# Routing of a one-core MoE layer: ties and counts by scans, slots summed once, the one-hot lanes in four strips, the first eight groups' row indices apart, and the register values of the expert loop by one load

## What is computed

```python
def hier_moe(x, p):                       # x: 640 tokens x 1024
    p_coarse = softmax(xt @ p['w_rc'] + p['b_rc'])            # 4 groups of experts
    p_grp, g_idx = lax.top_k(p_coarse, 1)                     # the first of equals wins
    l_fine = (xt @ p['w_rf'] + p['b_rf']).reshape(t, 4, 4)
    l_sel = take_along_axis(l_fine, g_idx[:, :, None], axis=1)[:, 0]
    top_l, e_idx = lax.top_k(l_sel, 2)                        # 2 experts of the group
    w_sel = softmax(top_l, axis=-1) * p_grp
    ...
    act = silu(xt @ w_gate[e]) * (xt @ w_up[e]) * gate        # 16 experts, 512 wide
    y = sum over e of act @ w_down[e]
```

## Time and profile before

| | us |
|---|---|
| median of 3 runs (1013.94 to 1014.93) | 1014.29 |
| the profiled execution | 1014.13 |
| its span, first to last instruction | 1012.0 |
| start of the routing on DVE (L1181), in the span | 660.94 |
| first matmul of the expert loop (L1743) | 693.42 |
| end of the last down matmul (L1754) | 965.86 |
| busy: PE / DVE / ACT / POOL | 867.5 / 410.3 / 264.3 / 103.9 |

### The profile page before, as it was taken

How to read it: one execution, slowest core, us unless ns; L and a number is a source line. 1 busy time by engine, 2 the same in 40 slices (tenths; PEclk the granted TensorE clock), 3 DMA queues, 4 the chain that set the end, 5 groups by cost and what they waited for, 6 DMA issues and landing times.

```text
span 1012.0 us, 17458 instructions
## 1 busy us (share of the span) xinstructions
PE 867.5 (86%) x6969; PEld 487.1 (48%) x6969; DVE 410.3 (41%) x792; ACT 264.3 (26%) x534; POOL 103.9 (10%) x199
## 2 busy tenths in 40 slices
PE   2998999999999999999874999635999999999910
PEld 0232455554454578444773445433555555555500
DVE  4445621222752922500564476261333333333345
ACT  0656311211110102121433132201333332333221
POOL 3100000000000000000101000002222222222140
PEclk9999999999999997989887999757999999999965
DMA  8964614043310020021203310595999999996162
GB/s 282 400 258 166 231 50 155 12 166 137 113 52 33 3 84 22 1 83 38 68 1 97 132 42 21 218 417 184 418 420 417 419 420 419 417 419 278 47 212 110
DMA packets 39850, 188.77 MB, mean 187 GB/s; under 512 B 4328, under 2 KB 4624, under 8 KB 32433
## 3 DMA queue, kind: packets, MB, share of 16 engines
q1 hardware_dynamic: 27754, 149.88, 37.2%
q0 software_dynamic: 8096, 26.34, 7.4%
q10 hardware_dynamic: 3944, 11.74, 3.2%
HBM read 171.52 MB, written 16.42 MB: 186 GB/s over the span
## 4 chain that ended last, share of the span: by engine, by line
PE 77%; DVE 11%; ACT 5%; DMA 3%; issue 2%; SPq 0%; POOL 0%; DVEq 0%; ACTq 0%; POOLq 0%
PE banks L1743 17%; PE banks L1458 14%; PE banks L1754 8%; PE banks L1593 7%; PE banks L1688 4%; PE banks L1459 3%; PE banks L1416 3%; PE banks L1499 3%; PE banks L1395 3%; PE banks L1354 2%; PE banks L1550 1%; PE banks L1531 1%; DMA arena<-in_hy_decay 1%; ACT arena L722 1%; PE banks L1762 1%
## 5 line engine op out<-in xcount | busy, mean ns | idle before, releaser
L1743 PE MATMUL banks<-arena 128*32 128x256 f32 x3072 | 177.7, 384 | 12.4 <-issue 12.4
L1458 PE MATMUL banks<-arena 128*128 128x512 f32 x320 | 164.2, 595 | 2.6 <-ACT arena L662 1.6
L1743 PEld LDWEIGHTS banks<-arena 128*32 128x32 f32 x3072 | 96.2, 111 | 76.7 <-issue 14.7
L1459 PEld LDWEIGHTS banks<-arena 128*128 128x128 f32 x320 | 60.8, 190 | 76.5 <-issue 76.5
L1754 PE MATMUL banks<-arena 128*32 128x256 f32 x1536 | 91.7, 379 | 1.0 <-DVE arena L1295 1.0
L1271 DVE STREAM_TRANSPOSE arena<-arena 128x256 f32<-128x256 f32 x49 | 32.3, 660 | 146.1 <-PE banks L1743 140.1
L1688 PE MATMUL banks<-arena 128*128 128x512 f32 x160 | 72.0, 609 | 1.7 <-DVE arena L1139 1.7
L1593 PE MATMUL banks<-arena 128*128 128x512 f32 x160 | 71.9, 612 | 0.0
L1754 PEld LDWEIGHTS banks<-arena 128*32 128x32 f32 x1536 | 50.0, 110 | 33.8 <-DVE arena L1295 1.2
L1459 PE MATMUL banks<-arena 128*128 128x128 f32 x320 | 61.5, 274 | 0.0
L1278 DVE COPY arena<-banks 32x256 f32<-32x256 f32 x98 | 41.5, 424 | 40.4 <-PE banks L1754 39.7
(11 more groups left out here) (355 smaller groups left out, 1029.8 us busy)
## 6 DMA issues: line engine op xcount, KB each, us to landing
arena<-in_w_gate SPq DMA_DIRECT2D x16, 2048.0 KB
arena<-in_w_up SPq DMA_DIRECT2D x16, 2048.0 KB
arena<-in_w_down SPq DMA_DIRECT2D x16, 2048.0 KB
arena<-in_w_ada SPq DMA_DIRECT2D x12, 2048.0 KB, 8.4
arena<-in_w_in SPq DMA_DIRECT2D x7, 2048.0 KB, 8.3
expert_output<-arena ACTq DMA_DIRECT2D x49, 128.0 KB
expert_output<-arena POOLq DMA_DIRECT2D x1, 4096.0 KB, 25.1
arena<-in_w_out SPq DMA_DIRECT2D x2, 2048.0 KB, 8.1
```

The costliest lines, as they stand in the source:

```text
L1458: M(ps[:, b, :], lhs, hT[:, k, CTX:TOK], start=k == 0, stop=k == KD - 1)
L1459: mm = M(ps[:, b + 1, 0:CTX], lhs, hT[:, k, 0:CTX], start=k == 0, stop=k == KD - 1)
L1743: mm = M(ps[q * LANE:(q + 1) * LANE, 2, 0:2 * P].rearrange("p (g f) -> p g f", g=2), xg[:, k, :], gate_up[e % 3][:, :, k, q * P:(q + 1) * ...
```

## The change

DVE prepares constants and zeroes before the logits are there: scan coefficients (one, and zero at the start of each row), a 128 x 128 matrix `fold` that is one where row and column agree modulo 32, `used` with a border column of 15.5/128, `cum`. Ties are broken by a running count (a scan) and one instruction that keeps the entry whose count is one. A scan over `used`, laid out expert by expert, gives the sums over the tiles ahead (`before`); PE adds `tri` times `used` and `ones` times `before` in one PSUM region and puts the totals in another, so the eight additions and two copies go. First group times 32 plus place is formed once (`at_slot`) and summed once. The lane mark `phot` is 32 columns wide; the ten matmuls write four strips of 32 partitions, which `fold` adds up and repeats (after a copy `parts` out of PSUM). This is done for groups 0 to 7 first, then for the other 64. `route_ready` counts two; the new `tiles_ready` stands for `tiles_i`, and SP, ACT and PE wait for it. PE reads the 17 values by one load, placed between the early and the late part; POOL waits for the second `route_ready` behind its first two gathers. Two setup semaphores are merged (`ld_ident` and `ld_rows` into `ld_setup`, `state_stored` into `out_stored`), with the sums waited for adapted; the shift of 15.5 goes into the table `late`.

```diff
+    late[:, 3 * P:4 * P] = i[None, :] % LANE + 15.5
...
+    fold, used, t_coef = area(W6 + 512, P), area(W6 + 640, NE, NT + 1), area(W6 + 736, NE, NT + 1)
+    e_coef, g_coef, cum = area(W6 + 832, NT, NE), area(W6 + 912, NT, NG), area(W6 + 932, NE + 1)
...
+    phot, early, later = rt(2 * NT, LANE), rt(2 * NT, EARLY), rt(2 * NT, GROUPS + 2 - EARLY)
...
-        sp.wait_ge(S["route_ready"], 1)
+        sp.wait_ge(S["tiles_ready"], 1)
...
         for n in range(2):
             pool.indirect_dma_start(xr[n], None, h2_quarters, bass.IndirectOffsetOnAxis(ap=idx_i[:, 1 + n:2 + n], axis=0))\
                 .then_inc(gather[n], 16)
+        pool.wait_ge(S["route_ready"], 2)
...
-        act.wait_ge(S["rt_v"], 1)
+        act.wait_ge(S["rt_v"], 3)
         link(A(rt_e, rt_e, ACT.Exp))
         link(A(rt_d, rt_d, ACT.Exp), "rt_exp")
 
 
-        act.wait_ge(S["route_ready"], 1)
+        act.wait_ge(S["tiles_ready"], 1)
...
+        def over(x, *dims):
+            return x.broadcast_to((P,) + dims)
...
+        lg, g1h, g_cnt, fine, e_cnt = rt(NT, 20), rt(NT, NG), rt(NT, NG), rt(NT, NE), rt(NT, NE)
...
+        for coef in (g_coef, e_coef, t_coef):
+            link(dve.memset(coef, 1.0))
+            link(dve.memset(coef[:, :, 0:1], 0.0))
+        link(dve.tensor_reduce(fold[:, 0:LANE], ident.rearrange("p (q r) -> p r q", q=LANES), AX_X, ALU.add))
+        link(CP(fold[:, LANE:].rearrange("p (q r) -> p q r", r=LANE), over(fold[:, 0:LANE].unsqueeze(1), LANES - 1, LANE)))
+        link(dve.memset(used, 15.5 / P))
+        link(dve.memset(cum, 1.0))
+
+        def flat(x):
+            return x.rearrange("p a b -> p (a b)")
+
+        def first_of_equals(hot, count, coef):
+
+            link(dve.tensor_tensor_scan(flat(count), flat(coef), flat(hot), 0.0, ALU.mult, ALU.add))
+            link(STT(hot, count, 1.0, hot, ALU.is_equal, ALU.mult))
+
...
         coarse = lg[:, :, 0:NG]
-        cmax, gmax, top1, top2, pg, rk = (rt(NT) for _ in range(6))
         link(dve.tensor_reduce(cmax, coarse, AX_X, ALU.max))
-        link(TT(rt_e, coarse, over(cmax.unsqueeze(2), NT, NG), ALU.subtract))
-        g1h = rt(NT, NG)
         link(TT(g1h, coarse, over(cmax.unsqueeze(2), NT, NG), ALU.is_equal))
-        link(TT(g1h, g1h, over(r4.unsqueeze(1), NT, NG), ALU.mult))
-        link(dve.tensor_reduce(gmax, g1h, AX_X, ALU.max))
-        link(TT(g1h, over(r4.unsqueeze(1), NT, NG), over(gmax.unsqueeze(2), NT, NG), ALU.is_equal))
+        first_of_equals(g1h, g_cnt, g_coef)
         link(TS(g1h, g1h, BIG, -BIG, ALU.mult, ALU.add))
-        fine = rt(NT, NE)
         link(TT(fine.rearrange("p t (g e) -> p t g e", g=NG), lg[:, :, NG:20].rearrange("p t (g e) -> p t g e", g=NG),
                 over(g1h.unsqueeze(3), NT, NG, EPG), ALU.add))
-        picks = rt(2, NT, NE)
         for c, top in enumerate((top1, top2)):
             e1h = picks[:, c]
             link(dve.tensor_reduce(top, fine, AX_X, ALU.max))
             link(TT(e1h, fine, over(top.unsqueeze(2), NT, NE), ALU.is_equal))
-            link(TT(e1h, e1h, over(r16.unsqueeze(1), NT, NE), ALU.mult))
-            link(dve.tensor_reduce(rk, e1h, AX_X, ALU.max))
-            link(TT(e1h, over(r16.unsqueeze(1), NT, NE), over(rk.unsqueeze(2), NT, NE), ALU.is_equal))
+            first_of_equals(e1h, e_cnt, e_coef)
             if c == 0:
                 link(STT(fine, e1h, -3.0 * BIG, fine, ALU.mult, ALU.add))
-        link(TT(used, picks[:, 0], picks[:, 1], ALU.add))
+        link(TT(used[:, :, 1:].rearrange("p e t -> p t e"), picks[:, 0], picks[:, 1], ALU.add), "rt_v")
+        link(dve.tensor_tensor_scan(flat(before), flat(t_coef), flat(used), 0.0, ALU.mult, ALU.add), "rt_v")
+        link(TT(rt_e, coarse, over(cmax.unsqueeze(2), NT, NG), ALU.subtract))
         link(TT(rt_d, top2, top1, ALU.subtract), "rt_v")
 
         dve.wait_ge(S["pos_done"], 1)
-        pos, tot = rt(NT, NE), rt(NT, NE)
-        link(CP(tot, ps[:, 6, 0:NT * NE].rearrange("p (t e) -> p t e", e=NE)))
-        link(CP(pos, ps[:, 5, 0:NT * NE].rearrange("p (t e) -> p t e", e=NE)))
-        for t in range(1, NT):
-            link(TT(pos[:, t, :], pos[:, t, :], tot[:, t - 1, :], ALU.add))
-            link(TT(tot[:, t, :], tot[:, t, :], tot[:, t - 1, :], ALU.add))
-
-        cnt, nt_f = tot[:, NT - 1, :], rt(NE)
-        link(TS(nt_f, cnt, 15.5, 1.0 / LANE, ALU.add, ALU.mult))
-        link(TS(nt_f, nt_f, MAGIC, None, ALU.add))
+        link(TS(nt_f, ps[:, 6, 0:NE], 1.0 / LANE, MAGIC, ALU.mult, ALU.add))
         link(TS(nt_f, nt_f, MAGIC, 2.0, ALU.subtract, ALU.max))
-        cum, odd, pair = rt(NE + 1), rt(1), rt(1)
-        link(dve.memset(cum, 1.0))
         link(dve.tensor_tensor_scan(cum[:, 1:NE + 1], ones[:, 0:NE], nt_f, 1.0, ALU.mult, ALU.add))
-        ck = rt(2, NT, NE)
-        pk, sl, grp = rt(2, NT), rt(2, NT), rt(2, NT)
-        link(TT(ck, picks, over(cum[:, 0:NE].unsqueeze(1).unsqueeze(1), 2, NT, NE), ALU.mult))
+        link(STT(at_slot.rearrange("p t e -> p e t"), over(cum[:, 0:NE].unsqueeze(2), NE, NT), float(LANE),
+                 ps[:, 5, 0:NT * NE].rearrange("p (e t) -> p e t", t=NT), ALU.mult, ALU.add))
+        link(TT(ck, picks, over(at_slot.unsqueeze(1), 2, NT, NE), ALU.mult))
         link(dve.tensor_reduce(sl, ck, AX_X, ALU.add))
-        link(TT(ck, picks, over(pos.unsqueeze(1), 2, NT, NE), ALU.mult))
-        link(dve.tensor_reduce(pk, ck, AX_X, ALU.add))
-        link(STT(sl, sl, float(LANE), pk, ALU.mult, ALU.add))
-        link(TS(grp, sl, -15.5, 1.0 / LANE, ALU.add, ALU.mult))
+        link(TS(grp, sl, -31.0, 1.0 / LANE, ALU.add, ALU.mult))
         link(TS(grp, grp, MAGIC, None, ALU.add))
         link(TS(grp, grp, MAGIC, None, ALU.subtract))
         link(STT(pk, grp, -float(LANE), sl, ALU.mult, ALU.add))
...
+        lane_id = rconst[:, RC - NT - 1:RC - NT]
+
+        def group_rows(hot, lo):
+            n = hot.shape[2]
+            link(TT(hot, over(groups[:, lo:lo + n].unsqueeze(1), 2 * NT, n), over(flat(grp).unsqueeze(2), 2 * NT, n),
+                    ALU.is_equal))
+            hot4 = hot.rearrange("p (c t) v -> p c t v", c=2)
+            link(TT(hot4, hot4, over(token.unsqueeze(1).unsqueeze(3), 2, NT, n), ALU.mult), "rt_v")
+
+        link(TT(phot, over(iota_row[:, 0:LANE].unsqueeze(1), 2 * NT, LANE), over(flat(pk).unsqueeze(2), 2 * NT, LANE),
                 ALU.is_equal))
-        for c in range(2):
-            v = vhot[:, c * NT:(c + 1) * NT, :]
-            link(TT(v, v, over(token.unsqueeze(2), NT, GROUPS + 2), ALU.mult), "rt_v")
-
-        link(CP(slot_i, sl))
+        group_rows(early, 0)
+
+        def gather_parts(lo, hi, done):
+            dve.wait_ge(S["idx_done"], done)
+            link(CP(parts[:, lo:hi], ps[:, 6, lo:hi]), "rt_v")
+
+        def row_indices(lo, hi, done):
+            dve.wait_ge(S["idx_done"], done)
+            link(TS(idx_i[:, lo:hi], ps[:, 3, lo:hi], lane_id, None, ALU.add), "route_ready")
+
+        link(TS(slot_i, sl, -15.5, None, ALU.add))
...
+        gather_parts(0, EARLY, 1)
...
         link(TT(cum[:, NE:NE + 1], cum[:, NE:NE + 1], odd, ALU.add))
         link(TT(nt_f[:, NE - 1:NE], nt_f[:, NE - 1:NE], odd, ALU.add))
+        row_indices(0, EARLY, 2)
         link(CP(tiles_i[0:1, 0:NE], nt_f[0:1, :]))
         link(CP(tiles_i[0:1, NE:NE + 1], pair[0:1, :]))
-        link(CP(tiles_i[0:1, 17:34], cum[0:1, :]))
-        dve.wait_ge(S["idx_done"], 1)
-        link(TS(idx_i, ps[:, 6, 0:GROUPS + 2], rconst[:, RC - NT - 1:RC - NT], None, ALU.add), "route_ready")
+        link(CP(tiles_i[0:1, 17:34], cum[0:1, :]), "tiles_ready")
+        group_rows(later, EARLY)
 
         dve.wait_ge(S["rt_exp"], 1)
-        w12 = rt(2, NT)
+        gather_parts(EARLY, GROUPS + 2, 3)
         link(dve.tensor_reduce(pg, rt_e, AX_X, ALU.add))
         link(TS(w12[:, 0], rt_d, 1.0, None, ALU.add))
         link(TT(w12[:, 0], w12[:, 0], pg, ALU.mult))
         link(dve.reciprocal(w12[:, 0], w12[:, 0]))
         link(TT(w12[:, 1], w12[:, 0], rt_d, ALU.mult))
+        row_indices(EARLY, GROUPS + 2, 4)
 
...
         pe.wait_ge(S["rt_v"], 1)
-        flat = used.rearrange("p t e -> p (t e)")
-        M(ps[:, 5, 0:NT * NE], tri, flat, start=True, stop=True)
-        M(ps[:, 6, 0:NT * NE], ones, flat, start=True, stop=True).then_inc(S["pos_done"], 1)
-        for n in range(2 * NT):
-            pe.wait_ge(S["rt_v"], 2 + n // NT)
-            mm = M(ps[:, 6, 0:GROUPS + 2], phot[:, n, :], vhot[:, n, :], start=n == 0, stop=n == 2 * NT - 1)
-        mm.then_inc(S["idx_done"], 1)
-        pe.wait_ge(S["route_ready"], 1)
+        M(ps[:, 5, 0:NT * NE], tri, used[:, :, 1:], start=True, stop=False)
+        pe.wait_ge(S["rt_v"], 2)
+        M(ps[:, 5, 0:NT * NE], ones, before[:, :, 0:NT], start=False, stop=True)
+        M(ps[:, 6, 0:NE], ones, before[:, :, NT], start=True, stop=True).then_inc(S["pos_done"], 1)
+
+        def row_numbers(hot, lo, ready):
+
+            pe.wait_ge(S["rt_v"], ready)
+            for n in range(2 * NT):
+                lane = n % LANES
```

(12 more changed lines are left out.)

47 lines of the change are left out of this document (22 added, 25 removed).

## The result

The kernel after has a median of 1011.11 us against 1017.35 us for the kernel before in the same series (18 runs each): a ratio of 0.9939, 95% interval 0.9923 to 0.9955, that is 6.2 us faster. The forecast was 11.7 us, in a range that began at 8.8. The direction and the place were right, the size was half of it, and the lower end of the range was missed too. (In absolute terms the median, 1011.11, stands beside the 1011.2 of rival (4). That is chance: the series' kernel before is 3.1 us slower than the runs that the forecast started from, and rival (4) had a gain of 3.1 us, not 6.2.)

A forecast was written before the change was run, and what follows sets the result against it. PE bounds the expert loop, so an earlier start ends it earlier: 7.6 us from indices plus 4.1 from register loads make 11.7, taking 1014.13 to 1002.4, as a median 1002.6; range 1000.4 to 1005.5.

The forecast's parts named there:

- rival (4): PE's register load: one load of 17 values costs what 17 loads cost, 12.0 us; time 1011.2; chance 0.05.
- What bounds the kernel now: Expert loop bound by PE; before it, gather and turn (8.1 us) and register loads (12.0) hang on the row indices.
- Choice of experts, counts, slots to early marks: DVE's routing up to PE's release: `used` at 665.5, restart after counts 667.2, early marks 670.8 instead of 676.51; 5.7 us gained.
- Early lanes: PE's 20 matmul records of 8 columns for groups 0 to 7: 1.6 us, between 1.1 and 2.1; indices at 673.85.
- two extra handovers: Between PE and DVE, from early marks to row indices: said to cost about 1.9 us of what shorter marks brought.
- Gather branch: POOL's first gather and DVE's turn: issue 0.8, gather 6.30 as before, rows turned at 681.7, give or take 1.5 us.
- Register branch: PE's one load, then 17 operations and checks at 0.07 to 0.22 us a pair; PE free at 676.7 to 679.2.
- Late part behind the load: Late lanes 1.6, copy 0.4, `fold` 0.86, L1258 0.3: late indices at 679.8 to 682.4, ahead of DVE's first turn.
- rival (1): Register operations keep 0.15 us each and the late part ends last: gain 10.3 us, time 1004.0; chance 0.22.
- Sum: First gate matmul at 681.7 instead of 693.42: 11.7 us, 7.6 from indices, 4.1 from register loads leaving the path.
- rival 2: PE's clock in the first group: higher level from the start gives 1000.6, wholly lower level 1003.7; chance 0.10.
- the first gate matmul right behind the turn: Sign expected in the profile after: PE starts the expert loop at about 681.7, once DVE has turned the gathered rows.

The follow-up runs named there:

- lanes_first: Kernel after with the late lanes and their `fold` matmul ahead of PE's register load; first routing instruction to first gate matmul 25.39 us, against 25.77 in the kernel after.
- lazy_gather_first: Kernel after with late lanes first, two register loads ahead and 15 in the loop, expert 2's weights requested only after two gathers landed; ratio to before 0.9934.

## Why the prediction was wrong

**What bounds the kernel now**: right. The loop is bound by PE and moves as a whole (272.4 and 272.2 us); two branches hang on the indices, and the register branch ends last.

**Choice of experts, counts, slots to early marks**: right to 0.1 us at each of the three marks (4.6, 6.3, 9.9 us forecast; 4.6, 6.2, 9.8 measured). The scans cost 0.20, 0.33 and 0.36 us where 0.24, 0.35 and 0.39 with the gap were charged.

**Early lanes**: too dear. 0.49 us instead of 1.6, and below my lower bound of 1.1. That bound took four weight loads of 32 columns at 0.22 us a round at the lower clock; with 8 columns behind each a round took 0.1. It was no lower bound: those 0.22 stood in a stream of 256-column matmuls, and the loads seem to have been held back by them. DVE wasn't even waiting when the result was there, so the indices came at 12.0 instead of 12.9. The sentence that the two extra handovers "cost about 1.9" has the sign wrong: by its own sum 3.05 us lie between PE's release and the indices, against 4.95 before. The 1.9 is a gain, and with the 5.7 it makes the 7.6.

**Gather branch**: 0.8 us from index to issue as forecast; but issue to turn 8.1 us in lanes_first instead of 6.3, outside my bound of 1.5. 0.45 of it is POOL's longer instruction. The rest I put down in the main to the traffic, since with the DMA engines nearly idle the rows were there within 4.6 (lazy_gather_first); why it is worse at this point of the weight stream than at the other wasn't tried. It hid behind the register branch here.

**Register branch**: the step that failed. "The load starts 0.44 after its release and the first register operation 1.04 after" carried the time of a load of one value (0.48) over to a load of seventeen. It took 4.2 us, 3.7 more, in the kernel before as well. And the upper bound of a pair of operation and check, 0.22, was too low: 0.29 in every kernel with one load, 1.2 us for 17. My own rows had room for that: of 0.66 us for each value the load is 0.30, which leaves 0.36 with the gaps and not 0.22. From tiles_ready to PE being free it was 9.2 us instead of at most 4.8 (the load also started at once and not 0.44 after its release). Rival (4) priced the load of a form that doesn't stand in the trace before, at 17 loads, but the sum's bounds left that open price out. The true value lies between: rival (4)'s mechanism at about three quarters of its price (9.2 of 12.0). No run shows the lower price of 0.07 for a pair either, on which the half that I took rested.

**Late part behind the load**: the form was right ("this is what is late next"): 4.0 us from PE's release to the first gate matmul, 3.9 by my sum. That the sum fits is luck: the late lanes took 1.0 us up to the copy and not 1.6, the copy with its gap 0.26 and not 0.4, and the place was filled by 0.53 us of idle before L1289 that the sum didn't have, by five small DVE instructions (1.0, where the sum had 0.86 for the `fold` matmul beside them) and by 0.2 more for the turn and the way to PE. By the code's order this idle holds the five semaphore increments ahead of DVE's first turn, which before ran in the shadow of the gather; that they are its cause wasn't tried. The late part ending last is also what rival (1) said; its sign, PE waiting on DVE after the gather, is there, but its gain of 10.3 us rested on the same short register branch.

**Sum**: 11.7 forecast, 6.7 measured. The indices brought 8.5 instead of 7.6; the registers and what stands behind them, which should have brought another 4.1, took 1.8 of that back. **Clock** (rival 2): 5.56 us for the first group against 5.71, at a granted clock of 0.65 and 0.63: next to nothing. The first groups of this study took 5.0 to 6.5 us.

**What would have shown it**: of the signs that I had named, "the first gate matmul right behind the turn" is true in the profile after and says nothing, since the turn itself waits for DVE's late indices.

## What to carry to other kernels

A combined instruction is a new instruction: take its price from a trace of that form, or keep both ends (one of the old, all of the old) in the sum. Register values that the loop needs one by one can be loaded in the loop (here 15 of them at no visible cost), and a list that must be loaded at once should start at an aligned word; a multiple of 16 is what these runs tried. When work is moved behind another step on an in-order engine, as the late lanes were, price it with that step at its dear end. A stream of transfers that is busy nine tenths of the time can have no room for a pause, even when its next use seems far off: here a pause of some 7 us came back as 7.4. And a stretch that ends just ahead of the clock's rise should be read together with the first group behind it.
